# Five RMS norms formed in two halves of 256 tokens between split products, and mixer parameters loaded during the FFN

## The reference, cut to what matters

```python
def rmsnorm(x, g, eps=NORM_EPS):
    xf = x.astype(jnp.float32)
    xf = xf * lax.rsqrt(jnp.mean(xf * xf, axis=-1, keepdims=True) + eps)
    return (xf * g.astype(jnp.float32)).astype(x.dtype)

def modulate(x, g, shift, scale):
    return rmsnorm(x, g) * (1 + scale) + shift

for i in range(DEPTH):                     # mixers: RWKV-7, SSD, attention, RWKV-7
    x = x + m[2] * mixer(modulate(x, norm1_g[i], m[0], m[1]))
    x = x + m[5] * conv_ffn(modulate(x, norm2_g[i], m[3], m[4]), ffn_w_in[i], ffn_conv[i], ffn_w_out[i])
```

## Time and profile before

| | |
|---|---|
| profiled execution | 4084.03 us, of which the span is 4082.4 |
| TensorE busy | 3886.9 us, 95% of the span |
| VectorE busy | 2279.3 us, 56% |
| ScalarE busy | 1279.6 us, 31% |
| GpSimd busy | 297.7 us, 7% |
| moved by DMA | 350.54 MB, mean 86 GB/s |
| mean granted clock of TensorE | 0.979 of full speed |

### The profile page before, as it was taken

The page is one execution under the profiler, slowest core; times in us unless marked ns, Lnnn a source line. Parts: engine busy times, 40 slices in busy tenths (PEclk is TensorE's granted clock), DMA queues, the critical chain, the costliest instruction groups (busy, mean ns, idle before and its releaser), DMA issues.

```text
span 4082.4 us, 82894 instructions
## 1 busy us (share of the span) xinstructions
PE 3886.9 (95%) x32635; PEld 2316.4 (57%) x32635; DVE 2279.3 (56%) x4094; ACT 1279.6 (31%) x2482; POOL 297.7 (7%) x246
## 2 busy tenths in 40 slices
PE   6999999999999999999999999999999999999999
PEld 2458778644444455544444445644444458888787
DVE  7837777466643566663666324456652427777432
ACT  3036665311100355540111014411100236666311
POOL 2001101000000132220000000000000000000000
PEclk9999999999999999999999999999999999999999
DMA  6610000044432332313444321044432220000254
GB/s 203 193 56 4 4 3 14 23 147 136 150 91 72 100 98 76 98 62 95 154 133 139 89 69 32 29 129 132 155 103 85 85 78 4 3 3 14 86 152 134
DMA packets 480998, 350.54 MB, mean 86 GB/s; under 512 B 24896, under 2 KB 450184, under 8 KB 478504
## 3 DMA queue, kind: packets, MB, share of 16 engines
q1 hardware_dynamic: 454680, 235.94, 20.1%
q0 software_dynamic: 26000, 110.06, 7.6%
HBM read 344.76 MB, written 1.18 MB: 85 GB/s over the span
## 4 chain that ended last, share of the span: by engine, by line
PE 79%; DVE 13%; ACT 5%; issue 1%; SPq 1%; DMA 1%; POOL 0%; DVEq 0%; ACTq 0%; POOLq 0%
PE PS L242 38%; PE PS L750 18%; PE PS L1710 14%; PE PS L850 2%; PE PS L425 2%; PE PS L898 1%; DVE WORK L2180 1%; DVE WORK L1451 1%; DVE WORK L1454 1%; DVE BIG L2242 1%; PE PS L1204 1%; DVE WORK L2299 1%; ACT WORK L1979 1%; PE PS L910 1%; ACT H L543 1%
## 5 line engine op out<-in xcount | busy, mean ns | idle before, releaser
L242 PE MATMUL PS<-H,WR 128*128 128x512 f32 (+1 forms) x3600 | 1425.2, 556 | 28.6 <-ACT H L543 23.9
L242 PEld LDWEIGHTS PS<-H,WR 128*128 128x128 f32 x3600 | 682.9, 191 | 726.1 <-issue 683.2
L750 PE MATMUL PS<-BIG,WR 128*128 128x512 f32 (+1 forms) x1984 | 770.8, 547 | 7.4 <-DVE BIG L1505 4.0
L1710 PE MATMUL PS<-WORK 64*64 64x64 f32 (+2 forms) x13088 | 571.5, 225 | 20.1 <-ACT WORK L1979 15.7
L750 PEld LDWEIGHTS PS<-BIG,WR 128*128 128x128 f32 x1984 | 374.0, 190 | 376.1 <-issue 353.2
L1710 PEld LDWEIGHTS PS<-WORK 64*64 64x64 f32 (+1 forms) x13088 | 479.7, 137 | 102.7 <-ACT WORK L1979 58.5
L418 DVE SCALAR_TENSOR_TENSOR WORK<-WORK,SC 128x512 f32<-128x512 f32 (+1 forms) x630 | 406.5, 645 | 22.4
L662 ACT ACTIVATE WORK<-PS,WORK 128x512 f32<-128x512 f32 (+1 forms) x176 | 111.5, 634 | 901.4 <-DVE WORK L690 522.8
L726 DVE SCALAR_TENSOR_TENSOR X<-PS,MOD,X 128x256 f32<-128x256 f32 x112 | 54.2, 484 | 497.8 <-PE PS L750 495.8
L1979 ACT ACTIVATE WORK<-PS 128x256 f32<-128x256 f32 (+3 forms) x720 | 243.6, 338 | 282.2 <-PE PS L1710 266.1
L675 DVE SCALAR_TENSOR_TENSOR WORK<-PS,WORK 128x510 f32<-128x510 f32 (+1 forms) x176 | 120.1, 682 | 316.1 <-ACT WORK L662 311.7
(11 more groups left out here) (254 smaller groups left out, 4289.1 us busy)
## 6 DMA issues: line engine op xcount, KB each, us to landing
WR<-in_ffn_w_in_dram SPq DMA_DIRECT2D x352, 256.0 KB, 2.9
WORK<-in_ada_w_dram POOLq DMA_DIRECT2D x33, 2048.0 KB, 9.1
WR<-in_ffn_w_out_dram SPq DMA_DIRECT2D x160, 256.0 KB, 2.7
WR<-in_ssd_w_in_dram SPq DMA_DIRECT2D x96, 256.0 KB, 2.8
WORK<-in_ada_w_dram POOLq DMA_DIRECT2D x16, 1024.0 KB, 5.8
BIG<-scratch_dram POOLq DMA_DIRECT2D x8, 2048.0 KB, 7.9
BIG<-in_ada_w_dram SPq DMA_DIRECT2D x4, 2048.0 KB, 18.5
WR<-in_rw_wk_dram SPq DMA_DIRECT2D x32, 256.0 KB, 2.8
```

The source lines that it names most:

```text
L242: mm = pe.matmul(outs, WR[:, slot, k, 0:m], rhs(k), start=first and k == 0, stop=last and k == nk - 1)
L750: mm = pe.matmul(PS[:, bank, lo:T], WR[:, opened[label], k, :], rhs(8 * r + k), start=r == 0 and k == 0, stop=last and k == nk - 1)
L1710: return pe.matmul(o, lhs, rhs, start=start, stop=stop)
```

## The change

Five norms (`n20`, `n11`, `n21`, `n12`, `n22`) are formed for tokens 0 to 255 and then for tokens 256 to 511. The other norms stay.

- The last output products before such a norm are split by tokens (`last_halves`): first halves of two weight units, then second halves, with both units held in `WR` meanwhile. The halves of a block go to two banks (`HALF_BANKS`). After four matmuls of the second half TensorE does the mean product of the first half (`half_mean_square`, bank 3). Blocks split: m = 6 and 7 after RWKV and attention, m = 7 after SSD and after an FFN (there its first unit goes through `first_part`).
- The first two products of the next stage are split in the same way (`first_halves`): first halves of both, second halves of both. The mean product of the second half comes after five matmuls of the first.
- VectorE adds the first half to X, forms some blocks k of the first half, adds the second half, forms the other blocks, and then forms the second half. ScalarE does Ln, Exp and its five blocks for one half and then for the other, with the table for Ln loaded ahead of each.
- The first iteration of the FFN loop on TensorE is written out ahead of the loop (`C.first`).
- GpSimd's loads for attention and SSD wait for the end of the mixer before, and so follow the riding loads of the FFN before.
- In SSD the wdt product goes to bank 5 and q = 2 of group 0 to bank 6; q = 1 and q = 2 come ahead of the transposes, q = 3 waits for conv 1, and the group's transposes wait for conv 2.

```diff
+        HALVED = {"n20": "mo0", "n11": "fo0", "n21": "mo1", "n12": "fo1", "n22": "mo2"}
+        MS_BANK = 3
+        HALF_BANKS = {"mo0": {6: (4, 6), 7: (5, 7)}, "mo1": {7: (1, 4)}, "mo2": {6: (7, 4), 7: (1, 5)}, "fo0": {7: (5, 6)},
+                      "fo1": {7: (5, 6)}}
+
+        def half_mean_square(tag, n):
+            pe.wait_ge(vec_done, sums_ready(HALVED[tag], n))
+            pe.matmul(PS[:, MS_BANK, SEGS[n]], const("mean"), SS[:, SEGS[n]], start=True, stop=False)
+            pe.wait_ge(vec_done, C.at(f"{HALVED[tag]}.sq{n}"))
...
+        def last_halves(tag, units, rhs, r_last):
...
+            for n in range(2):
+                for j, (m, r, nk) in enumerate(units):
+                    label = f"{tag}.w{m}{r}"
+                    for k in range(nk):
+                        if n == 0 and k % 4 == 0:
+                            pe.wait_ge(w_loaded[2 * slots[j] + k // 4], C.at(f"{label}.{k // 4}"))
+                        mm = pe.matmul(PS[:, HALF_BANKS[tag][m][n], SEGS[n]], WR[:, slots[j], k, :],
+                                       rhs(8 * r + k)[:, SEGS[n]], start=r == 0 and k == 0, stop=r == r_last and k == nk - 1)
+                        if n and k == 3:
+                            mm.then_inc(w_used, C.mark(w_used, None))
+                            if j == 0:
+                                half_mean_square(halved_tail[tag], 0)
...
+        def first_halves(tag, units):
...
+            for n in range(2):
+                for j, (label, i, out, cols) in enumerate(units):
+                    for k in range(KD):
+                        if n == 0 and k % 4 == 0:
+                            pe.wait_ge(w_loaded[2 * slots[j] + k // 4], C.at(f"{label}.{k // 4}", i))
+                        if j == 0:
+                            pe.wait_ge(act_done if k in BY_ACT else vec_done, C.at(f"{tag}.h{k}{n}"))
+                        mm = pe.matmul(out[:, SEGS[n]], WR[:, slots[j], k, 0:cols], Hk[:, k, SEGS[n]], start=k == 0,
+                                       stop=k == KD - 1)
+                        if n and k == 3:
+                            mm.then_inc(w_used, C.mark(w_used, None))
+                        if (n, j, k) == (0, 0, 4):
+                            half_mean_square(tag, 1)
...
+        def half_norm_act(tag, prev, gain, shift):
+            table(act, LOGS)
+            act.wait_ge(vec_done, C.ended(vec_done, f"{prev}.front"))
...
+            for n in range(2):
+                if n:
+                    table(act, LOGS)
+                act.wait_ge(pe_done, C.at(f"{tag}.ms{n}"))
+                s(act.activation(RS[:, SEGS[n]], PS[:, MS_BANK, SEGS[n]], ACT.Ln, bias=MC[:, 0:1]))
+                s(act.activation(RS[:, SEGS[n]], RS[:, SEGS[n]], ACT.Exp, scale=-0.5), f"{tag}.rs{n}")
+                for k in BY_ACT:
+                    act.wait_ge(vec_done, C.at(f"{tag}.t{k}{n}"))
+                    s(act.activation(Hk[:, k, SEGS[n]], TMP[k][:, SEGS[n]], ACT.Identity, scale=MS[:, gain, k, n:n + 1],
+                                     bias=shift(k, n)), f"{tag}.h{k}{n}")
...
+                    vec.wait_ge(pe_done, C.at(f"fo{l}.half{m}"))
+                    add_half(m, 0, PS[:, HALF_BANKS[f"fo{l}"][m][0], :], l, 5, f"fo{l}")
+                    half_norm_vec(f"n1{l + 1}", 0, range(3), 2 * l + 2, mod_shift(l + 1, 0))
+                    vec.wait_ge(w_used, C.at(f"fo{l}.w{m}2.used"))
+                    add_half(m, 1, PS[:, HALF_BANKS[f"fo{l}"][m][1], :], l, 5, f"fo{l}")
+                    half_norm_vec(f"n1{l + 1}", 0, range(3, KD), 2 * l + 2, mod_shift(l + 1, 0))
+                    break
...
+                    for n in range(2):
+                        for m in halved:
+                            vec.wait_ge(*((w_used, C.at(f"{tag}.w{m}{r}.used")) if n else (pe_done, C.at(f"{tag}.half{m}"))))
+                            add_half(m, n, PS[:, HALF_BANKS[tag][m][n], :], l, 2, tag)
+                            if n and m == KD - 2 or r and not n:
+                                norm(range(4))
+                    norm(range(4, KD))
+                    break
...
         def attn_pool(l):
-            enter(pool, (), f"n1{l}")
+            enter(pool, (pool_done,), f"mix{l - 1}")
...
+        def input_bank(n, q):
+            return 6 if (n, q) == (0, 2) else q % 2
...
-            use_unit(None, "ssd.wdt", PS[0:64, 0, :], lambda k: Hk[:, k, :], 8, True, True, 64, normed(f"n1{l}"))
-            gemm(0, 0)
+            first_halves(f"n1{l}", [("ssd.wdt", None, PS[0:64, 5, :], 64), ("s0." + UNITS[0], None, PS[:, 0, :], P)])
+            leave((pe_done, w_used), f"n1{l}")
             gemm(0, 1)
+            gemm(0, 2)
             pe.wait_ge(vec_done, C.at("ssd.acs"))
...
-            for q in range(2, 5):
+            for q in range(3, 5):
                 gemm(0, q)
+            pe.wait_ge(vec_done, C.at("s0.cv2"))
             transposes(0)
```

More of the change, by code:

```diff
@@ L109, in loop, with first @@
     @contextmanager
-    def loop(self, eng, name, trips):
+    def first(self, name):
+        now, marks = dict(self.now), dict(self.marks)
+        self.loop_name = name
+        yield 0
+        self.now, self.marks, self.loop_name = now, marks, None
+    @contextmanager
+    def loop(self, eng, name, trips, start=0):
         before = dict(self.now)
         self.loop_name = name
-        with eng.Fori(0, trips) as i:
+        with eng.Fori(start, trips) as i:
             yield i
@@ new lines, in side_ended @@
+        def side_ended(eng, stage):
+            for sem_ in (act_done, pool_done):
+                if C.ended(sem_, stage) > 0:
+                    eng.wait_ge(sem_, C.ended(sem_, stage))
+        def last_halves(tag, units, rhs, r_last):
+            slots = []
+            for _ in units:
+                slots.append(C.now.get("w_unit_pe", 0) % 2)
+                C.mark("w_unit_pe", None)
+            for n in range(2):
[11 more added lines that the diff above has]
+                    if n:
+                        mm.then_inc(w_used, C.mark(w_used, label + ".used"))
+                    elif r == r_last:
+                        mm.then_inc(pe_done, C.mark(pe_done, f"{tag}.half{m}"))
@@ new lines, in first_part @@
+        def first_part(tag, m, rhs):
+            slot = C.now.get("w_unit_pe", 0) % 2
+            C.mark("w_unit_pe", None)
+            pe.wait_ge(vec_done, part_done(tag, m - 2))
+            for k in range(KD):
+                if k % 4 == 0:
+                    pe.wait_ge(w_loaded[2 * slot + k // 4], C.at(f"{tag}.w{m}0.{k // 4}"))
+                for n in range(2):
+                    mm = pe.matmul(PS[:, HALF_BANKS[tag][m][n], SEGS[n]], WR[:, slot, k, :], rhs(k)[:, SEGS[n]],
+                                   start=k == 0, stop=False)
+                if k % 4 == 3:
+                    mm.then_inc(w_used, C.mark(w_used, f"{tag}.w{m}0.used" if k == KD - 1 else None))
@@ L549, in norm_vec @@
         def norm_vec(tag, prev, lo, gain, shift):
+            if tag in HALVED:
+                half_norm_vec(tag, 1, range(KD), gain, shift)
+                leave((vec_done,), tag)
+                return
             enter(vec, (vec_done,), prev)
@@ L618, in ffn_pe, with rest @@
         def ffn_pe(l, lo):
[L619 to L625, removed]
+            def rest(i, units, ready=None):
+                for q, h in units:
+                    if q or h:
+                        pe.wait_ge(vec_done, C.at(f"f{l}.cv{q}{h}", i, 1))
+                    use_unit(i, f"f{l}.w{q}{h}", PS[:, 2 * q + h, lo:T], lambda k: Hk[:, k, lo:T], 8, True, True,
+                             ready=None if q or h else ready)
                 if l + 1 < DEPTH:
@@ L628, in ffn_pe @@
                 pe.wait_ge(vec_done, C.at(f"f{l}.cv00", i))
+            four = [(q, h) for q in range(2) for h in range(2)]
+            if f"n2{l}" in HALVED:
+                C.mark(pe_done, f"n2{l}.ms1")
+                with C.first(f"f{l}") as i:
+                    first_halves(f"n2{l}", [(f"f{l}.w0{h}", i, PS[:, h, :], P) for h in range(2)])
+                    leave((pe_done, w_used), f"n2{l}")
+                    rest(i, four[2:])
+                with C.loop(pe, f"f{l}", NF // 2, 1) as i:
+                    rest(i, four)
+            else:
+                with C.loop(pe, f"f{l}", NF // 2) as i:
+                    rest(i, four, normed(f"n2{l}"))
             pe.wait_ge(vec_done, C.at(f"f{l}.g1", NF // 2 - 2))
@@ L763, in parts_vec @@
                     add_squares(SQB, lo)
+                if tag in halved_tail and m == KD - (1 if r else 2):
+                    halved = (m,) if r else (m, m + 1)
+                    norm = lambda ks: half_norm_vec(f"n2{l}", 0, ks, 2 * l + 1, mod_shift(l, 1))
+                    leave((vec_done,), f"mix{l}.front")
+                    side_ended(vec, f"mix{l}")
+                    for n in range(2):
+                        for m in halved:
[5 more added lines that the diff above has]
+                    break
```

81 lines of the change are left out of this document (63 added, 18 removed).

## The result

The changed kernel takes 4058.61 us in the median of five runs (4052.88 to 4064.43), beside 4084.14 for the kernel before (five runs). The ratio is 0.9937, 95% interval 0.9923 to 0.9952: 25.5 us faster where I had forecast 40.8, and 2.6 us above the upper end of my range. The profiled execution took 4054.67 us with a span of 4053.0.

What follows compares the result with a forecast made beforehand. TensorE's products bound the kernel, with 59.7 us lost at five norms. Gains 5.8 + 7.5 + 5.8 + 13.4 + 9.2 - 0.9 = 40.8 us gave 4042 us against the runs' median; range 4032 to 4056.

Steps and rivals of the forecast that it cites:

- The subtraction that gave 59.7 us: At five norms, TensorE's elapsed time less its full-rate work: 59.7 us of stops and slow running.
- the price of split products: Two 256-column records cost about one of 512; splitting adds 0.2 us per boundary, 0.9 in all.
- the steps inside the norm before an FFN: Worked timeline of a halved norm: 0.63 and 1.65 us lost, 2.3 left of 8.12 and of 8.06.
- RS hidden in the first half: Halved norm before an FFN: first RS ready at 11.81 while the second halves last until 14.69.
- the 0.1 to 0.6 I had: Expected sign: TensorE waits of 0.1 to 0.6 us at k = 4 and the second half's first k.
- My 9.2 for SSD: Norm before SSD: 8.7 us (2.5 + 4.7 + 1.5) left of 17.98, gain 9.2.
- from the end W of the wdt product: In SSD, TensorE has 17.9 us of work from W, conv 1 comes at W + 22.6: 4.7 us lost.
- rival 5: A later stage takes the gain back, as with FFN riding sums some 3 us later: 4080, chance 0.03.
- rivals 1 to 3: Weights late (4055, chance 0.11), dearer table switches (4055, 0.03), halves at the whole norm's pace (4057, 0.06).
- Late weights: Three FFN norms each lose 4.3 us to a late weight transfer: 13 us, 4055, chance 0.11.
- Dearer table switches: Table switches ahead of second-half RS cost twice their row: 12.8 us later, 4055, chance 0.03.
- rival 4: Paced second halves and alternating banks lower the clock at five norms: 73.5 us, 4116, chance 0.03.

Runs made afterwards that it cites:

- the early counts: Changed kernel with the counts telling other engines TensorE has left a norm taken right after the second mean product: 4046.44 us, ratio 0.9914.
- the counts one product later: Changed kernel with the FFN's leave counts taken after its third product, in three FFNs only: 4083.52 us, ratio 1.0004.
- one more SSD product: The early counts, plus SSD's q = 3 of group 0 in bank 5 ahead of the small transposes: 4043.57 us, ratio 0.9903.
- SSD's order of before: The early counts, but SSD's q = 2 back behind the small transposes, in q = 0's bank, waiting for conv 0: 4046.10 us, ratio 0.9913.
- five blocks: One more SSD product, plus VectorE forming blocks k = 0 to 4 of the first half before the second half's add: 4040.07 us, ratio 0.9900.

## Why the prediction was wrong

**Right, and shown.** The subtraction that gave 59.7 us, the price of split products, and the steps inside the norm before an FFN: RS hidden in the first half, 0.59 us at k = 4, the second half at the pace of ScalarE and VectorE, a table load with no idle time behind it, no weight wait on a split product, the clock at full. Before SSD and attention the first half stops at k = 3 instead, for 0.91 and 0.97 us, more than the 0.1 to 0.6 I had. With the early counts the stretch fell by 40.8 us, the forecast to the tenth, and that is partly luck. Place by place that kernel gained 5.4, 6.9 and 5.4 us before the three FFNs, 12.9 before attention and 7.6 before and in SSD, where I had 5.6, 7.3, 5.6, 13.2 and 9.0 with the split products' 0.2 taken off: 38.2 in all. The other 2.6 lie in the same two parts, where the kernel before has two half-clock stretches that this one trace has not (see "The rest"). My 9.2 for SSD should have been 9.3 by its own terms. Attention's and SSD's parameters gave 9.8 us by themselves, in the middle of the 9 to 10 expected.

**The step that failed** is the one that said, before SSD, that "from the end W of the wdt product" the chain of 18.1 us starts, and, for the FFN, that only a smaller delay of the riding sums was to be feared (3 us, in rival 5). I read the waits that the added functions contain and did not read what the moved `leave` does to the stage behind it. Z could not start at W; it waited for the second half of x0. From 1327.47 to 1350.72 are 23.25 us where 13.74 + 0.70 are work: 8.8 lost instead of 4.7. Three FFNs lost 0.92 us each in the first iteration, and layer 1's then ran at half clock: its 64 records took 29.43 us instead of 27.73. Attention lost 0.91. Together 4.1 + 2.8 + 1.7 + 0.9 = 9.5 of the 13.3 us. The early counts took these stops away or back to size, and the counts one product later made them grow, so this cause is shown.

**The rest.** Of the other 3.8 us, 3.1 are half-clock time further on in attention's part. Another half-clock stretch stands in SSD. Windows of the changed kernel, then the same places with the early counts, then with one more SSD product, which has the early counts too:

```profile
1400.00:1410.00 10.00, 9.28 (x46) 0.83 0.60 235
2449.00:2457.00 8.00, 6.93 (x19) 0.57 0.01 3
```

```profile
1391.00:1401.00 10.00, 9.09 (x50) 1.00 0.68 252
2435.00:2443.00 8.00, 6.61 (x34) 1.00 0.01 3
```

```profile
1392.00:1402.00 10.00, 8.37 (x44) 0.83 0.60 236
2438.00:2446.00 8.00, 7.48 (x28) 0.79 0.01 3
```

So these two don't need the late counts. They stand in the kernel before as well (granted clock 0.83 in 1405 to 1415, 0.79 in 2470 to 2478) and with SSD's order of before (0.83 in 1399 to 1409, 0.79 in 2445 to 2453); of the traces with halved norms only the early counts alone and five blocks have 1.00 at both. What decides whether they come, and why the one in attention is longer in the first trace of the changed kernel than in its second, stays open.

**The rivals.** Late weights did not come: no wait on weights stands in the split products. Dearer table switches did not come either. The Trainium skill (ScalarE: Activation LUTs, "What ACT_TABLE_LOAD costs") has a drain of about 1380 ns for each switch. The timeline of ScalarE, at the switch from Ln to Exp in a second half, disagrees: the load starts 0.03 us after Ln ends and Exp 0.01 us after the load:

```profile
835.13 0.47 ACT L607 ACTIVATE WORK<-PS,MC 128x256 f32<-128x256 f32 x1
835.63 1.28 ACT L608 ACT_TABLE_LOAD   x1
836.92 0.42 ACT L608 ACTIVATE WORK<-WORK 128x256 f32<-128x256 f32 x1
```

The clock did not fall within the norms, so rival 4 (slower than before) was wrong. Rival 5 was the right kind of loss, work behind the norm that starts late, at the wrong chance (0.03) and with the wrong cause. My range was too narrow on that side: its upper end came from losses inside the norms and rivals 1 to 3, with nothing for the stage behind them.

## What to carry to other kernels

When work is pulled across a stage's boundary, look at what the engines of the next stage wait for, not only at the new waits: a mark "this stage is over" that moves with the pulled work holds every other engine back, although it changes no instruction. Such a cost shows as idle time ahead of an engine's first instruction of a stage, released by an engine whose result that instruction doesn't read. Where whole runs wander, compare a stretch of the trace that holds the change and leaves the wandering part out, and divide it: a gain that lies in a part where the edit can't act isn't the edit's.

## What I had not expected of the hardware

Identical instructions took different times up to the first changed one: it started at 810.59 us in one trace and at 819.29 in another. Over the stretch behind it the changed kernel's two traces agree within 2 us, though their parts don't. And a stop of 0.91 us, which costs little by itself, was followed by a granted clock of 0.57 in 1944 to 1948, so that at layer 1's FFN the half-speed work cost more (29.43 - 27.73 = 1.7 us) than the stop. After the same stop in layers 0 and 2 the clock stayed full in that trace; in the second trace of the same kernel it fell after all three (0.79 in 862 to 870, 1944 to 1952 and 2700 to 2708). The same stop costs 0.9 or 2.6 us from one execution to the next.
